# The scale 1/rms of four norms moved from a matmul's inputs to its products, and the attention output put in buffers of its own

## What is computed

```python
def rms_norm(x, g):
    y = x * lax.rsqrt(jnp.mean(x * x, axis=-1, keepdims=True) + EPS)
    return y * g

h = rms_norm(x, norm_mix_g[0]);  qkv = h @ w_qkv_a            # 1024 -> 3072
#   q, k: rms_norm over 64, rope;  differential attention A (softmax), rms_norm over 128
x = x + o @ w_o_a
x = x + swiglu(rms_norm(x, norm_ffn_g[0]), w_gate_up[0], w_down[0])
k_s, v_s = split(rms_norm(x, kv_norm_g) @ w_kv_s)              # shared K and V
q = rms_norm(x, norm_mix_g[1]) @ w_q_b                         # stick-breaking attention B
x = x + o @ w_o_b
x = x + swiglu(rms_norm(x, norm_ffn_g[1]), w_gate_up[1], w_down[1])
```

## Time and profile before

| | before |
|---|---|
| median of 3 runs | 1898.03 us (1895.55 to 1898.28) |
| the profiled execution, its own time | 1897.06 us |
| its span in the profile | 1895.4 us |
| PE matmuls busy | 1766.9 us, 93% |
| VectorE busy | 789.8 us, 42% |
| ScalarE busy | 613.7 us, 32% |
| GpSimd busy | 25.5 us, 1% |
| memory traffic | 258.42 MB, mean 136 GB/s |

### The profile page before, as it was taken

The page is one execution under the profiler, slowest core; times in us unless marked ns, Lnnn a source line. Parts: engine busy times, 40 slices in busy tenths (PEclk is TensorE's granted clock), DMA queues, the critical chain, the costliest instruction groups (busy, mean ns, idle before and its releaser), DMA issues.

```text
span 1895.4 us, 33046 instructions
## 1 busy us (share of the span) xinstructions
PE 1766.9 (93%) x14548; PEld 1635.6 (86%) x14548; DVE 789.8 (42%) x896; ACT 613.7 (32%) x917; POOL 25.5 (1%) x48
## 2 busy tenths in 40 slices
PE   3999999988899999999979998888879999999998
PEld 3999766668899999999979995555779999999998
DVE  6664266654523223223451215777554222223222
ACT  4333355552322122112232315666423211221120
POOL 0000000000000000000000000000000000000000
PEclk9999999999899999999989998999989999999999
DMA  4123699951121211212213347998311211212211
GB/s 162 45 85 126 234 370 375 380 198 67 57 77 67 90 67 66 89 67 71 100 52 123 122 156 260 360 357 325 112 45 68 86 70 67 89 67 78 78 67 78
DMA packets 37812, 258.42 MB, mean 136 GB/s; under 512 B 4416, under 2 KB 4544, under 8 KB 8384
## 3 DMA queue, kind: packets, MB, share of 16 engines
q1 hardware_dynamic: 33984, 245.15, 34.6%
q0 software_dynamic: 3712, 11.54, 1.8%
HBM read 242.51 MB, written 13.11 MB: 135 GB/s over the span
## 4 chain that ended last, share of the span: by engine, by line
PE 81%; DVE 12%; ACT 3%; issue 2%; DMA 1%; SPq 0%; ACTq 0%; DVEq 0%
PE ps L375 60%; PE ps L190 4%; PE ps L191 4%; PE ps L192 4%; DVE rows L985 2%; DVE pw L953 2%; PE ps L640 2%; PE ps L689 1%; DVE h_lo L244 1%; DVE pp L957 1%; PE ps L593 1%; DVE work L258 1%; PE ps L609 1%; DVE rows L254 1%; PE ps L597 1%
## 5 line engine op out<-in xcount | busy, mean ns | idle before, releaser
L375 PE MATMUL ps<-h_hi,w_hi 128*128 128x320 f32 x1920 | 444.6, 313 | 34.5 <-DVE h_lo L244 30.3
L375 PE MATMUL ps<-h_lo,w_hi 128*128 128x320 f32 x1920 | 441.6, 312 | 0.0
L375 PE MATMUL ps<-h_hi,w_lo 128*128 128x320 f32 x1920 | 440.9, 311 | 0.0
L375 PEld LDWEIGHTS ps<-h_hi,w_hi 128*128 128x128 f32 x1920 | 324.5, 190 | 40.3 <-issue 35.2
L375 PEld LDWEIGHTS ps<-h_lo,w_hi 128*128 128x128 f32 x1920 | 325.1, 190 | 0.0
L375 PEld LDWEIGHTS ps<-h_hi,w_lo 128*128 128x128 f32 x1920 | 324.7, 190 | 0.0
L182 DVE TENSOR_TENSOR w_lo<-w_raw,w_hi 128x2048 fp32r<-128x2048 f32 x100 | 229.1, 2291 | 201.7 <-ACT w_hi L174 201.7
L174 ACT ACTIVATE w_hi<-w_raw 128x2048 fp32r<-128x2048 f32 x100 | 190.6, 1906 | 205.4 <-PE ps L375 204.3
L190 PE MATMUL ps<-w_hi,h_hi 128*128 128x256 f32 x640 | 184.7, 289 | 12.7 <-DVE h_lo L244 11.8
L473 DVE TENSOR_TENSOR gu<-ps,sg 128x640 f32<-128x640 f32 x44 | 36.3, 824 | 363.9 <-PE ps L375 363.9
L191 PE MATMUL ps<-w_lo,h_hi 128*128 128x256 f32 x640 | 182.7, 285 | 0.0
(11 more groups left out here) (157 smaller groups left out, 1730.8 us busy)
## 6 DMA issues: line engine op xcount, KB each, us to landing
w_raw<-in_w SPq DMA_DIRECT2D x100, 1024.0 KB, 4.8
kv<-in_v_a SPq DMA_DIRECT2D x22, 1024.0 KB, 7.7
kv<-in_v_s SPq DMA_DIRECT2D x22, 1024.0 KB, 7.0
kv<-in_k_a SPq DMA_DIRECT2D x20, 1024.0 KB, 7.3
kv<-in_k_s SPq DMA_DIRECT2D x20, 1024.0 KB, 7.4
work<-in_k_a SPq DMA_DIRECT2D x12, 1024.0 KB, 7.9
work<-in_k_s SPq DMA_DIRECT2D x12, 1024.0 KB, 8.1
work<-in_v_a SPq DMA_DIRECT2D x10, 1024.0 KB, 8.0
```

The source lines that it names most:

```text
L375: last = nc.tensor.matmul(ps[:, bank0 + 2 * n + h, 0:HALF], w[:, k, n * P:(n + 1) * P], m[:, k, h * HALF:(h + 1) * HALF], start=(k == 0 an ...
```

## The change

The inputs of the four norms with a weight (qkv, FFN 0, k/v with q of layer B, FFN 1) are no longer multiplied by 1/rms. `h_hi` is `xT * g` and `h_lo` the rest of it, made right behind each residual add. The factor 1/rms comes from the same sum of squares, now by Ln and Exp on ScalarE (`root`), as a row over the tokens (`rstd_row`) or as a column per token tile (`rstd_col`), and is multiplied in where the products leave PSUM: in FFN on VectorE into the gate (before silu) and into the silu (before the product with up); for K and Q of layer B on VectorE (`kq_dve`, which replaces ScalarE's `kq_act`); for qkv and V as the scale of ScalarE's evacuation.

The sums' matmuls are put inside the first unit after the norm (`mid`). The attention output has `o_hi` and `o_lo`, which lie over `qkp` and `v5`; so these must be stored first, and the V store of layer A is cut in four and moved ahead of attention A. The q inputs of layer B go into `h2_hi` while ks runs and, tile by tile, into `h_lo` while the last vs unit frees it. At the start the first weight unit and x are loaded before the constants, the first unit goes k by k over all token tiles, and GpSimd adds up the squares of the first norm. Attention B's ring begins with another buffer. y is stored in four pieces.

```diff
+        norm = sems("norm", "sq sum hi lo ms ln rstd cms cln cols")
+        total, rstd_row, rstd_col = rows[:, 0, :], rows[:, 1, :], st[:, 64:64 + TT]
+            def hi(self, act, t, x_ready):
+                act.wait_ge(*x_ready)
+                nc.scalar.activation(h_hi[:, t, :], xT[:, t, :], ACT.Copy, scale=self.g(t)).then_inc(norm["hi"], 1)
+            def lo(self, dve, t):
+                dve.wait_ge(norm["hi"], self.n * KT + t + 1)
+                nc.vector.scalar_tensor_tensor(h_lo[:, t, :], xT[:, t, :], self.g(t), h_hi[:, t, :].bitcast(F32),
+                                               ALU.mult, ALU.subtract).then_inc(norm["lo"], 1)
+            def pe(self, pe, bank):
+                pe.wait_ge(norm["sum"], (self.n + 1) * (KT - 1))
+                if self.cols:
+                    for t in range(TT):
+                        last = nc.tensor.matmul(ps[:, bank + 2, t:t + 1], total[:, t * P:(t + 1) * P], ones[:, 0:1],
+                                                start=True, stop=True, skip_group_check=True)
+                    last.then_inc(norm["cms"], 1)
+                if self.rows:
                     for h in range(2):
-                        last = nc.tensor.matmul(ps[:, h, 0:HALF], ones[:, :],
-                                                rows[:, 0, h * HALF:(h + 1) * HALF], start=True, stop=True)
-                    last.then_inc(self.s["ms"], 1)
+                        last = nc.tensor.matmul(ps[:, bank + h, 0:HALF], ones[:, :],
+                                                total[:, h * HALF:(h + 1) * HALF], start=True, stop=True)
+                    last.then_inc(norm["ms"], 1)
+            def root(self, act, bank):
+                if self.cols:
+                    act.wait_ge(norm["cms"], self.col_n + 1)
+                    nc.scalar.activation(rstd_col, ps[:, bank + 2, 0:TT], ACT.Ln, bias=eps, scale=1.0 / D)\
+                        .then_inc(norm["cln"], 1)
+                    act.wait_ge(norm["cln"], self.col_n + 1)
+                    nc.scalar.activation(rstd_col, rstd_col, ACT.Exp, scale=-0.5).then_inc(norm["cols"], 1)
+                if self.rows:
+                    act.wait_ge(norm["ms"], self.row_n + 1)
+                    nc.scalar.activation(rstd_row.rearrange("p (h n) -> p h n", h=2), ps[:, bank:bank + 2, 0:HALF],
+                                         ACT.Ln, bias=eps, scale=1.0 / D).then_inc(norm["ln"], 1)
+                    act.wait_ge(norm["ln"], self.row_n + 1)
+                    nc.scalar.activation(rstd_row, rstd_row, ACT.Exp, scale=-0.5).then_inc(norm["rstd"], 1)
...
@@ token_unit @@
+            if h_ready is not None:
+                for k in range(KT - 1):
+                    pe.wait_ge(h_ready[0], h_ready[1] + k + 1)
+                    for t in range(TT):
...
+                        product(t, k)
+                pe.wait_ge(h_ready[0], h_ready[1] + KT)
+                for t in range(TT):
+                    product(t, KT - 1).then_inc(mm, 1)
+                if mid is not None:
+                    mid()
+                return
...
@@ residual_act / residual_dve, where a norm follows @@
+                    for n in range(2):
+                        norm.hi(act, j * 2 + n, (x_done, j * 2 + (x0 + n + 1)))
...
+                    for n in range(2):
+                        norm.lo(dve, j * 2 + n)
                     for n in range(2):
                         norm.accumulate(dve, j * 2 + n)
...
@@ ffn_act @@
-                    nc.scalar.activation(sg[:, s, :].rearrange("p (h c) -> p h c", h=2), banks(0),
-                                         ACT.Silu).then_inc(ff["gate"], 1)
+                    act.wait_ge(ff["gate"], j + (f0 + 1))
+                    nc.scalar.activation(sg[:, s, :], sg[:, s, :], ACT.Silu).then_inc(ff["silu"], 1)
@@ ffn_dve @@
                     split_lo(dve, ph, j + (j0 + 1), 1 - s)
-                    dve.wait_ge(ff["gate"], j + (f0 + 1))
+                    dve.wait_ge(mm, tiles_before(ph, j + j0) + 1)
+                    nc.vector.tensor_tensor(sg[:, s, :].rearrange("p (h c) -> p h c", h=2), banks(0),
+                                            rstd_row.rearrange("p (h c) -> p h c", h=2), ALU.mult)\
+                        .then_inc(ff["gate"], 1)
+                    dve.wait_ge(ff["silu"], j + (f0 + 1))
+                    nc.vector.tensor_tensor(sg[:, s, :], sg[:, s, :], rstd_row, ALU.mult).then_inc(ff["sr"], 1)
...
@@ block.sync @@
-            for k in range(2):
-                load(k, k)
+            load(0, 0)
+            for i in range(4):
+                sp_.dma_start(xT[:, 2 * i:2 * i + 2, :], a_x[:, 2 * i:2 * i + 2, :]).then_inc(loaded[f"x{i}"], 16)
+            load(1, 1)
+            sp_.dma_start(const[:, :], a_const).then_inc(loaded["const"], 16)
...
-            tb.loads(sp_, [[(Norm.s["lo"], 4 * KT)], [(mm, tiles_before("qb", 3))], [(mm, tiles_before("ob", 0))]])
+            tb.loads(sp_, [[(mm, tiles_before("qb", 3))], [(mm, tiles_before("ob", 0))], []])
...
-            sp_.wait_ge(x_done, KT * 8)
-            sp_.dma_start(o_y, xT[:, :, :]).then_inc(stored, 16)
+            for i in range(4):
+                sp_.wait_ge(x_done, KT * 7 + 2 * i + 2)
+                sp_.dma_start(o_y[:, 2 * i:2 * i + 2, :], xT[:, 2 * i:2 * i + 2, :]).then_inc(stored, 16)
@@ block.gpsimd @@
+            for t in range(KT):
+                norms["mix0"].accumulate(pool, t)
...
+            for j in range(4):
+                pool.wait_ge(qk["ev"], (9 + j) * TT)
+                settle(pool)
+                nc.gpsimd.dma_start(o_va[:, j * UC:(j + 1) * UC].rearrange("(t p) c -> p t c", p=P),
+                                    v5[:, :, j * UC:(j + 1) * UC]).then_inc(qk["vstored"], 16)
+            ta.pool(pool, [(mm, tiles_before("oa", 0))])
@@ block.scalar, behind the last unit of ff0 @@
+            for j in range(4):
+                split_hi(act, "ks", j + 1, 1 - j % 2)
+                if j == 0:
+                    norms["kv"].root(act, 4)
+                    act.wait_ge(norm["cols"], 2)
+                for t in range(2 * j, 2 * j + 2):
+                    nc.scalar.activation(h2_hi[:, t, :], xT[:, t, :], ACT.Copy, scale=norms["kv"].g(t, G_MIX1))\
+                        .then_inc(mix1["hi"], 1)
@@ block.vector, behind the vs units @@
+            for t in range(KT):
+                dve.wait_ge(mix1["hi"], t + 1)
+                dve.wait_ge(*((mix1["free"], t + 1) if t < KT - 1 else (mm, tiles_before("qb", 0))))
+                nc.vector.scalar_tensor_tensor(h_lo[:, t, :], xT[:, t, :], norms["kv"].g(t, G_MIX1),
+                                               h2_hi[:, t, :].bitcast(F32), ALU.mult, ALU.subtract)\
+                    .then_inc(mix1["lo"], 1)
```

More of the change, by code:

```diff
@@ L227, in act @@
-            def act(self, act, h_free):
-                s = self.s
-                if not self.again:
-                    act.wait_ge(s["mean"], self.full + 1)
-                    nc.scalar.activation(rows[:, 1, :], rows[:, 1, :], ACT.Sqrt).then_inc(s["std"], 1)
-                act.wait_ge(*h_free)
-                for t in range(KT):
-                    if not self.again:
-                        act.wait_ge(s["y"], self.full * KT + t + 1)
-                    nc.scalar.activation(h_hi[:, t, :], work[:, t, :], ACT.Copy, scale=self.g(t))\
-                        .then_inc(s["hi"], 1)
@@ L281, in token_unit @@
                 for k in range(KT):
-                    if h_ready is not None and t == 0:
-                        pe.wait_ge(h_ready[0], h_ready[1] + k + 1)
-                    last = mm3(ps[:, t, 0:UC], h_hi[:, k, t * P:(t + 1) * P], h_lo[:, k, t * P:(t + 1) * P],
-                               w_hi[s][:, k, :], w_lo[s][:, k, :], k == 0, k == KT - 1)
+                    last = product(t, k)
+                    if k_done is not None and t == TT - 1 and k < KT - 1:
+                        last.then_inc(k_done, 1)
                 last.then_inc(mm, 1)
@@ L379, in feature_unit @@
                 last.then_inc(mm, 1)
+                if n == 0 and mid is not None:
+                    mid()
         def banks(b):
@@ L1156, in program, with kq_pe @@
         kq = sems("b", "kev vev qev kstored vstored")
-        def kq_pe(pe, ph, ev, h_ready, ready=()):
-            def step(j, s):
-                first = isinstance(j, int) and j == 0
+        mix1 = sems("mix1", "hi lo free")
+        def kq_pe(pe, ph, ev, m_hi, m_lo, h_ready, ready=(), mid=None):
+            for j in range(4):
+                first = j == 0
                 frees = [None, None] if first else [(ev, j * 2 - 1), (ev, j * 2)]
-                feature_unit(pe, ph, j, s, h_hi, h_lo, KT, 0, frees, ready if first else (),
-                             h_ready=h_ready if first else None)
-            in_pairs(pe, 4, step)
```

296 lines of the change are left out of this document (144 added, 152 removed).

## The result

| | before | after |
|---|---|---|
| median | 1896.79 us, 4 runs (1894.87 to 1898.28) | 1831.75 us, 4 runs (1831.18 to 1832.37) |
| span of the profiled execution | 1895.4 us | 1830.0 us |
| GpSimd busy | 25.5 us | 41.6 us |

What follows compares the result with a forecast made beforehand. TensorE bounds the kernel, so only its gaps count. Norms 43.5, qb 3.3 less 0.4, start 16.7 and end 4.1 sum to 67.2 us off 1897.06: 1829.9, predicted as 1830, range 1820 to 1842.

Steps and rivals of the forecast that it cites:

- The three norms: Gaps before FFN 0, k/v and FFN 1: 16.6, 16.6 and 17.1 us go, less what comes back; 43.5 us gained together.
- 1/rms behind the first unit: After the three norms: 1/rms in time by 0.4 us at FFN 0, about 1 us late at k/v and FFN 1.
- The case that the loads vanish by themselves: Table loads inside Ln/Exp pairs: joint sets save 3 us; part of the cheaper case, 1821 us, chance 0.15.
- the one of 2.7 us each: Five exposed ScalarE table loads at 2.7 us each add 7 us: 1837 us; shares chance 0.13 with slow GpSimd adds.
- The end: Store of y: only 640 KB left after the last add instead of 2560 KB; gain 4.1 us, bounds 3 to 5.
- qb: Norm before qb: tiles made while vs is multiplied, saving 3.3 us; K and Q leaving over VectorE cost 0.4.
- FFN steady state: The 44 FFN units: two more VectorE products each, 5.6 us of work in 14.08 us of PE work; cost 0.
- the slower rival: FFN units: VectorE late in every one; at 2 us a unit 1918 us; chance 0.02.
- The start: Kernel start to unit 1: it begins at 33.8 instead of 52.7, less 2.2 for the clock; gain 16.7 us, bounds 11 to 22.
- the late rival: 1/rms later than thought: GpSimd adds at 2.5 us each, or dearer ScalarE function changes; 1837 us, chance 0.13.
- The attentions: Attentions A and B: cost 0 from passed queues and the new buffer order; at B bound 6 us late.
- rival of 12 us at B: Attention B: 2.1 MB less prefetched; if its ring cannot catch up, PE waits 6 us early and again later; 1842, chance 0.06.

Runs made afterwards that it cites:

- The inputs made late: Changed kernel, but before FFN 0, k/v and FFN 1 `h_hi` and `h_lo` of all tiles are made only after the last add: 1846.50 us, ratio 0.974.
- four more products: Changed kernel plus four more overwritten 640-column VectorE products in each of the 44 FFN units: 1829.71 us, one run.

## Why the prediction was right

*The three norms.* Forecast 15.4, 13.2 and 14.9 us, measured 15.7, 13.1 and 15.1. The price of a gap as the distance between where PE could have been and where it flows again, and not as the wait that the view of waits adds up, was the right one. The plain waits add up to 30.3 us on `h_lo` and three times 2.6 on the sums, 38 in all, where the prediction counted 50.3 and took off 6.8 for what comes back; 43.9 were gained. That contains the low clock, too, as the windows at 1.00 show. The inputs made late show how it splits: 30 us for the serial norm, 14 for the inputs.

*1/rms behind the first unit.* FFN 0 was to have it in time by 0.4 us and has no wait; FFN 1 and k/v were to wait about 1.0 each and wait 0.9 and 1.1. The assumption that Exp after Ln needs a load is shown by the three loads in the timeline, and their price by what naming the set gave back. The case that the loads vanish by themselves is refuted, and so is the one of 2.7 us each.

*The end.* Forecast 4.1, measured 4.6 between the profiles and 4.5 with the edit undone alone. The span ends 4.1 us behind the start of the last add; the forecast of 4.7 was 0.6 long. A 640 KB store from SP's queue takes 2.9 us from issue to landing where the earlier trace rows had 4.2 for one from GpSimd's queue.

*qb.* Forecast 3.3 less 0.4, measured 3.0.

*FFN steady state.* Free, as forecast: units stand 14.08 us apart, and four more products are free too. But the reckoning behind it was a wrong one that happened to suffice. It added up busy time, 5.6 us, plus 0.7 for silu; the chain is 8.2. By the prediction a unit had room for 7.8 us more (14.08 less 6.3); it has 5.9, and past that the cost is more than the 44 times the lateness by which the slower rival was priced.

*The start* is the term that was mis-sized: 14.0 against 16.7. The 2.7 us are wholly in the place at which unit 1 begins, 36.49 instead of 33.8. The squares were done 0.3 early, the additions took 14.35 us instead of 11.2, the ten column products 1.28 instead of 1.2, and from there to unit 1 it was 0.2 less. The clock's part was right: from unit 1 to attention A before 220.51 - 52.7 = 167.8 us, after 206.49 - 36.49 = 170.0, so 2.2 us more. What went into the additions: with nothing beside it one takes 1.53 us and the next follows 1.67 after its start, where 1.6 was assumed; beside VectorE's rope products it is 1.84; and the first lost 2.0 us to VectorE's `w_lo`. The prediction had put both beside the additions as free. It had named additions outside 0.6 to 1.8 us as a sign of being wrong, and by that sign this step was: the first was 3.57, and the seven took 2.05 each, halfway from the 1.6 of the sum to the 2.5 of the late rival. It named "three streams" as a reason for a high price, but did not look for whose instruction would be under way. One miss cost nothing: PE began at 12.77 instead of 11.7, because ScalarE loaded a table (1.28 us from 6.30) ahead of its first `w_hi`; the sum was ready last, so it stayed hidden.

*The attentions.* Forecast 0 in both, with a rival of 12 us at B. Attention B gained 0.2 and shows no new wait: the ring catches up. By its scatter, though, a total within 2 us of the forecast is closer than one profile can promise, and that much of the agreement is luck.

## What to carry to other kernels

When a chain stands between two matmul phases, price it as the time at which TensorE flows again less the time at which it could have, clock included; a factor that commutes with the product (1/rms here) can be applied to the results while only its cheap part stays on the inputs. What hides an edit is the other engine's slack along its whole chain of waits, so subtract that chain from the period, not the busy time. Where ScalarE changes between Ln and Exp, name the table that has both, and where GpSimd and VectorE are both to read two operands from SBUF, reckon with one of them standing still while the other's instruction lasts.

## What the runs showed of the hardware

- *VectorE and GpSimd stop each other.* An addition of 640 columns on GpSimd took 1.53 us alone, about 1.7 beside rope products, and 3.57 when it began under a `w_lo` that ran until 20.40; `w_lo` took 2.29 us alone and 3.65 across additions; a rope product of 160 columns took 0.31 us and, across an addition, 1.69. In all three the one that came later was longer by nearly the rest of the other. The Trainium skill, "SBUF — State Buffer", section "🔬 SBUF: two separate sides", has it that a VectorE instruction with two SBUF inputs and a GpSimd instruction that reads SBUF exclude each other for a whole instruction; these rows agree. By it, moving `w_lo` among the additions can't help, and moving it behind them does, as measured at the place (0 and 1.7 us).
- *The clock after a short pause is not the same each time.* At the start of the kernel after it held behind 3.4 us of idle time and fell in the 2.4 us behind the ten column products (1.00 from 32 to 34, 0.59 from 34 to 36, 0.50 from 36 to 38). In two runs it was still at 1.00 when a pause of 1.1 us began behind these products; it fell behind the pause in one (0.62 from 34 to 38) and held in the other. Of three pauses of 3.5 us in one run it held behind the first and fell behind the other two. No row here settles what decides it. From unit 1 to attention A the run whose clock held took 167.95 us, those in which it fell 169.2 to 170.6.
- *A copy out of PSUM with a factor per partition* took 0.47 us on ScalarE where the plain one took 0.38.
